# Differential attention: the squares of a head's output and their row sums on GpSimd instead of ScalarE and VectorE

## The reference, cut to what matters

```python
s = jnp.einsum('bqhcd,bkhcd->bhcqk', qb, k).astype(jnp.float32)
p = jax.nn.softmax(jnp.where(mask, s, -jnp.inf), axis=-1)
a = p[:, :, 0] - lam * p[:, :, 1]
o = jnp.einsum('bhqk,bkhe->bqhe', a.astype(v.dtype), v)      # 512 rows x 128 per head
...
o = rms_norm_2(o, subln_g) * (1.0 - lam_init)                 # per row and head: mean of 128 squares
return o.reshape(B, S, H * DIFF_V_DIM) @ w_out
```

## Time and profile before

| what | value |
|---|---|
| three runs, each one execution | 2382.07, 2386.46, 2394.81 us, median 2386.46 us |
| span of the profiled execution | 2382.2 us |
| the profiled execution's own time | no figure beside its span is given for it; the fastest run is 0.13 us under the span |
| TensorE busy | 2355.2 us, 99% of the span |
| VectorE, ScalarE, GpSimd busy | 798.0, 853.5 and 1162.4 us |
| chain that ended last, by engine | PE 88%, DVE 7%, issue 2% |
| the attention loop of the differential attention | about 1264 to 1352 us of the span |

### The profile page before, as it was taken

The page is one execution under the profiler, slowest core; times in us unless marked ns, Lnnn a source line. Parts: engine busy times, 40 slices in busy tenths (PEclk is TensorE's granted clock), DMA queues, the critical chain, the costliest instruction groups (busy, mean ns, idle before and its releaser), DMA issues.

```text
span 2382.2 us, 27151 instructions
## 1 busy us (share of the span) xinstructions
PE 2355.2 (99%) x11234; PEld 1924.9 (81%) x11234; DVE 798.0 (33%) x1384; ACT 853.5 (36%) x1266; POOL 1162.4 (49%) x960
## 2 busy tenths in 40 slices
PE   8999999999999999999999999999999999999999
PEld 7888887888887788888887678888887777788887
DVE  3222205854212322100466742022046863410210
ACT  4222214514342322212446543223156463431330
POOL 6544446634554544444452365444556822644443
PEclk9999999999999999999999999999999999999999
DMA  4323233212332323232220122233232201322322
GB/s 147 106 89 105 89 100 113 89 54 71 124 122 67 95 89 106 89 106 89 85 92 19 54 89 91 104 90 105 89 103 67 75 1 54 94 102 91 96 96 89
DMA packets 147521, 210.54 MB, mean 88 GB/s; under 512 B 6203, under 2 KB 113862, under 8 KB 147398
## 3 DMA queue, kind: packets, MB, share of 16 engines
q1 hardware_dynamic: 147398, 208.80, 27.2%
HBM read 206.69 MB, written 2.10 MB: 88 GB/s over the span
## 4 chain that ended last, share of the span: by engine, by line
PE 88%; DVE 7%; issue 2%; POOL 1%; DMA 1%; ACT 1%; SPq 0%; DVEq 0%; POOLq 0%; ACTq 0%
PE ps L1465 27%; PE ps L1467 26%; PE ps L1466 26%; PE ps L2243 2%; DVE c_work L2964 1%; DVE c_best L2963 1%; DVE small L2807 1%; PE ps L2221 1%; POOL wlo L759 1%; PE ps L2231 1%; PE ps L1726 1%; PE ps L1794 1%; POOL sq L774 1%; PE ps L1816 1%; DVE hl L2380 1%
## 5 line engine op out<-in xcount | busy, mean ns | idle before, releaser
L759 POOL TENSOR_TENSOR wlo<-raw,whi 128x512 fp32r<-128x512 f32 x776 | 1007.0, 1329 | 1082.9 <-ACT whi L952 981.8
L952 ACT ACTIVATE whi<-raw 128x2048 fp32r<-128x2048 f32 (+1 forms) x185 | 352.4, 1905 | 688.2 <-DMA raw<-in_mlp_w 317.1
L1465 PE MATMUL ps<-hh,whi 128*128 128x512 f32 x1448 | 572.9, 396 | 6.6 <-DVE hl L2380 5.4
L1467 PE MATMUL ps<-hh,wlo 128*128 128x512 f32 x1448 | 566.3, 391 | 0.0
L1466 PE MATMUL ps<-hl,whi 128*128 128x512 f32 x1448 | 566.3, 391 | 0.0
L1465 PEld LDWEIGHTS ps<-hh,whi 128*128 128x128 f32 x1448 | 273.5, 189 | 73.1 <-issue 9.3
L1467 PEld LDWEIGHTS ps<-hh,wlo 128*128 128x128 f32 x1448 | 273.3, 189 | 57.7
L1466 PEld LDWEIGHTS ps<-hl,whi 128*128 128x128 f32 x1448 | 273.7, 189 | 56.8 <-issue 1.2
L1466 PE MATMUL ps<-gl,whi 128*128 128x512 f32 x736 | 286.4, 389 | 0.0
L1465 PE MATMUL ps<-gh,whi 128*128 128x512 f32 x736 | 286.3, 389 | 0.0
L1467 PE MATMUL ps<-gh,wlo 128*128 128x512 f32 x736 | 286.3, 389 | 0.0
(11 more groups left out here) (448 smaller groups left out, 2920.1 us busy)
## 6 DMA issues: line engine op xcount, KB each, us to landing
raw<-in_mlp_w SPq DMA_DIRECT2D x64, 1024.0 KB, 5.5
raw<-in_ffn_w_up SPq DMA_DIRECT2D x22, 1024.0 KB, 5.1
raw<-in_ffn_w_down SPq DMA_DIRECT2D x22, 1024.0 KB, 4.8
raw<-in_ffn_w_gate SPq DMA_DIRECT2D x21, 1024.0 KB, 5.1
raw<-in_w_in SPq DMA_DIRECT2D x13, 1024.0 KB, 5.1
raw<-in_diff_w_in SPq DMA_DIRECT2D x12, 1024.0 KB, 5.0
raw<-in_xattn_w_kv SPq DMA_DIRECT2D x8, 1024.0 KB, 5.2
raw<-in_dsa_w_in SPq DMA_DIRECT2D x8, 1024.0 KB, 5.0
```

Source lines behind the costliest of these rows:

```text
L759: nc.gpsimd.tensor_tensor(wlo[i][:, c], raw[i][:, c], whi[i][:, c].bitcast(F32), ALU.subtract).then_inc(s_lo, 1)
L952: nc.scalar.activation(whi[i][:, 0:width(made[0])], raw[i][:, 0:width(made[0])], ACT.Copy)\
L1465: nc.tensor.matmul(dst, w_hi, x_hi, start=start, stop=False)
L1467: return nc.tensor.matmul(dst, w_lo, x_hi, start=False, stop=stop)
```

## The change

For heads 0 to 6, GpSimd makes the squares and their sums: one multiplication 128x512 of `d_o` with itself, six halving additions (256, 128, 64, 32, 16 and 8 results per partition), a seventh that leaves the four sums, and the scale to `newton`. Every one of the nine waits for the one before it. They stand ahead of `head_scaled(h)` in GpSimd's program. ScalarE's `squares` and VectorE's `row_sums` leave the loop and stay for head 7 alone, behind it. ScalarE's `factors(h)` waits for `s_dovar` as before, which GpSimd now raises.

```diff
@@ GpSimd
             def diff(b):
                 split_to(b + DIFF_BLOCKS - 1)
                 for h in range(8):
+                    if h < 7:
+                        head_squares(h)
                     head_scaled(h)
                     if h in (0, 5, 6):
                         split_to(b + DIFF_BLOCKS + (0, 5, 6).index(h))
+
+            def head_squares(h):
+
+                o, rows = d_o[:, h % 2, :], d_osq[:, :].rearrange("p (t e) -> p t e", e=P)
+                pool.wait_ge(s_dor, h + 1)
+                nc.gpsimd.tensor_tensor(d_osq[:, :], o, o, ALU.mult).then_inc(s_dosq, 1)
+                pool.wait_ge(s_dosq, 8 * h + 1)
+                n = P // 2
+                while n > 1:
+                    nc.gpsimd.tensor_tensor(rows[:, :, 0:n], rows[:, :, 0:n], rows[:, :, n:2 * n], ALU.add)\
+                        .then_inc(s_dosq, 1)
+                    pool.wait_ge(s_dosq, 8 * h + 9 - n.bit_length())
+                    n //= 2
+                nc.gpsimd.tensor_tensor(small[:, 24:28].unsqueeze(2), rows[:, :, 0:1], rows[:, :, 1:2], ALU.add)\
+                    .then_inc(s_dosq, 1)
+                pool.wait_ge(s_dosq, 8 * h + 8)
+                nc.gpsimd.tensor_scalar(newton[:, 0, 0:4], small[:, 24:28], -0.5 / P, -0.5 * EPS, ALU.mult, ALU.add)\
+                    .then_inc(s_dovar, 1)
@@ ScalarE, squares(h), now called for head 7 alone
                     act.wait_ge(s_dor, h + 1)
-                    if h:
-                        act.wait_ge(s_doss, h)
+                    act.wait_ge(s_dovar, h)
                     nc.scalar.activation(d_osq[:, :], d_o[:, h % 2, :], ACT.Square).then_inc(s_dosq, 1)
@@ ScalarE, the loop over u
                     if qt == 0 and h >= 2:
                         high(h - 2)
-                    if qt == 1 and h:
-                        squares(h - 1)
                     if qt == 2 and h:
                         factors(h - 1)
@@ VectorE, row_sums(h), now called for head 7 alone
-                    dve.wait_ge(s_dosq, h + 1)
+                    dve.wait_ge(s_dosq, 8 * h + 1)
...
-                    dve.wait_ge(s_doss, h + 1)
+                    dve.wait_ge(s_doss, 1)
@@ VectorE, the loop over u
                     if qt == 0 and h:
                         rows_copy(h - 1)
-                    if qt == 1 and h:
-                        row_sums(h - 1)
```

## The result

The changed kernel takes 2393.54 us (median of 20 runs, 2389.34 to 2395.43), the kernel before 2386.11 us (median of 20 runs beside it, 2381.81 to 2394.81). The ratio is 1.003 with a 95% interval of 1.0023 to 1.0036: slower by 5.5 to 8.6 us, less than 0.5%. The forecast was 6.6 us, and 2390.9 us.

A forecast was written before the change was run, and what follows sets the result against it. TensorE, busy 99% of the span, bounds the kernel. Head terms sum to +6.6 us on a 2382.2 us span, giving 2388.8; half the 4.3 us distance to the median makes 2390.9, range 2384 to near 2398 and 2 more.

The forecast's parts named there:

- ScalarE's part: ScalarE loses 0.62 us in seven heads; nothing is gained, as it waits for VectorE anyway.
- VectorE's part: Without row sums and scale on VectorE, the reciprocal starts earlier, limited by ScalarE's exponentials: 0.22 us gained per head.
- 4.6 us without meetings: GpSimd's nine linked operations from VectorE's rows to the raised semaphore, no collision with VectorE; lower bound 4.3 us.
- L = 5.3: GpSimd's chain length in us from VectorE's rows to the semaphore, with two d_a meetings at 0.36 us each.
- (b): Rival: GpSimd blocked for VectorE's whole instruction at every meeting; chain 5.7 to 6.07 us, +9.4 to +12 us, chance 0.18.
- L + 2.82: Time in us from VectorE's rows to TensorE's transposes: chain length, then factors 0.52, scaling 2.18, two handovers 0.12.
- L - 5.00: Change of head 3's cycle in us, repeated in heads 2 and 4, never below -0.22; forecast +0.30 each.
- +1.81: Head 1's added us: its squares start 1.11 us late behind a low part in GpSimd's program.
- L - 2.11: Head 6's added us: squares behind a low part delay ScalarE's last d_aT copy for TensorE; forecast +3.19.
- (a): Rival: short chain of 4.3 to 4.9 us, collisions of tenths; +2 to +4 us, about 2388, chance 0.25.
- (c): Rival: small dependent additions cost about 0.56 us each, chain near 7.3 us; +20.6 us, 2405, chance 0.08.
- (d): Rival: margins absorb everything, heads 1 and 6 don't pay for the low part; -1.5 us, 2383 to 2385, chance 0.04.

The follow-up runs named there:

- experiment 10: Kernel before with squares on GpSimd, sums kept on VectorE, second block's low part behind head 6's scaling; loop stretch 84.59 us, ratio to kernel before 0.9991.
- Experiment 7: Changed kernel with the halving additions of 128 to 8 results left out, a short chain; loop stretch 86.13 us, ratio to kernel before 1.0000.
- experiment 6: Changed kernel with two more dependent 128x4 operations in GpSimd's chain; loop stretch 96.63 us, ratio to kernel before 1.0061.
- experiment 4: Kernel before with first block's low part in halves behind heads 1 and 2, second's behind head 6's scaling; loop stretch 85.69 us, ratio 1.0008.
- experiment 2: Changed kernel with the first block's low part made in halves behind heads 1 and 2; loop stretch 92.04 us, ratio to kernel before 1.0036.
- experiment 1: Changed kernel with the second block's low part moved behind head 6's scaling; loop stretch 88.70 us, ratio to kernel before 1.0017.
- Experiment 9: Kernel before with only the second block's low part moved behind head 6's scaling; loop stretch 84.59 us, median 2381.62 us, ratio 0.9995.
- experiment 5: Changed kernel with only the squares on GpSimd, sums back on VectorE in the loop; loop stretch 88.24 us, ratio to kernel before 1.0003.
- experiment 8: Changed kernel with three of four low-part pieces before head 6's squares, the last behind its scaling; head 5 to 6 19.98 us, ratio 1.0034.

## Why the prediction was right

**What the change removes.** ScalarE's part at nothing: shown by experiment 10. VectorE's part at 0.22 us a head: the mechanism was right (the reciprocal ends a wait for ScalarE), its size was not. Experiment 7 shows 0.09 in heads 2 to 4 (and 0.36 in head 5), and head 0 in the changed kernel +0.02: the d_a for 128 keys meets GpSimd's scaling, a meeting that the working did not look for. It took VectorE's waits as some tenths, behind operations of 0.46 us and less, and left out the scaling, which takes 1.04.

**The chain.** 4.6 us without meetings was too long. The squares took 1.04 us and not 1.30 (both inputs are the same tensor), as the lower bound of 4.3 had it. The six additions with their gaps were sized right, at 2.58: in experiment 6, head 2, where nothing held them, they took 2.57. With the sum, the scale and the handovers that makes 4.3.

```profile
1307.01 2.57 POOL L872 TENSOR_TENSOR d_osq<-d_osq 128x256 f32<-128x256 f32 x6
```

**The meetings.** L = 5.3 was measured as 5.22 in heads 2 to 4. The two meetings came where the working put them, with the d_a for 384 and for 512 keys, but at 0.33 and 0.54 us and not at 0.36 each. So they cost 0.87 us and not 0.72, the chain without them 4.35 and not 4.6, and the two errors nearly cancel: that L came out within 0.1 us is in part luck. What a meeting cost followed from what was left of the other's instruction, less 0.13 to 0.20 us: 0.33 of 0.47 and 0.54 of 0.67 us for GpSimd in head 2, 0.58 of 0.78 for VectorE behind the scaling there, 1.12 of 1.32 in experiment 4. The Trainium skill's page "SBUF — State Buffer" (section "Who interferes with whom") states that issue order decides who blocks, and that the other is blocked for the whole instruction. The traces agree with the second part, up to those 0.13 to 0.20 us. With the first they agree in head 2; in experiment 4 VectorE's d_a started 0.05 us before GpSimd's piece by the trace and waited for it all the same. I had read that rule as a whole instruction for each meeting, rival (b); what counts is what is left of it.

**Who waits.** L + 2.82 to the transposes gives 1300.47 + 8.04 = 1308.51 in head 2; they came at 1308.81, since TensorE first had to transpose the d_a that the scaling held up. This 0.30 us, too, no step of the working had, and against it the rows come sooner after the transposes of the head before. In head 3: from rows to transposes 8.34 us for 7.82, of which 0.22 are L - 5.00 and 0.30 the d_a; from head 2's transposes to the rows 3.11 us for 3.28; together +0.35 for +0.30. Experiment 6 shows the slope of one per head in heads 3 to 6.

**Head 1.** +1.56 for +1.81; experiment 2 shows that the place caused 1.21 of it, a part of that through the meeting with the d_a for 384 keys (1.09 us in place of 0.62), which the sum had not. TensorE's wait lay elsewhere than I said: not at the transposes of d_o until GpSimd, but in two parts ahead of them, until ScalarE's exponentials, which stand behind the factors, and until the d_a for 128 keys:

```profile
1295.46 0.92 PE L1958 MATMUL ps<-a_kT,a_qT 64*128 64x384 f32 x4 [0.82 <-ACT d_p L1269]
...
1297.19 0.33 PE L1999 MATMUL ps<-ident,d_a 128*128 128x128 f32 x1 [0.82 <-DVE d_a L2837]
```

**Head 6.** +3.19 forecast, +3.43 measured, of unlike parts. From VectorE's rows the last copy is 8.12 us off (1354.61 - 1346.49) where it was 5.49 (1350.39 - 1344.90): +2.63, near L - 2.11 for the 4.85 us of this chain. The rows themselves came 0.64 us earlier after the transposes of head 5 (3.38 for 4.02): d_a for 256 keys took 0.75 us and not the 1.41 of the earlier trace rows, since the first piece of the low part had begun 0.80 us before it (1343.68 and 1344.48) and not 0.14. And the low clock added 1.44, which no step of mine had. So this term, nearly half of the sum, came near by luck.

**The signs.** The total of the chain, its two stretched operations, the reciprocal that waits for ScalarE and the gap of some 3 us in head 6 were as forecast. TensorE's 1 to 2 us of waiting in heads 1 and 5 were there in size (1.64 and 1.58), not in place. Of the signs of being wrong, "VectorE and not GpSimd stretches" came half true: both stretch, VectorE's d_a for 128 keys by 0.58 us in heads 2 to 4.

**The rivals.** (a), (b) and (c) name lengths of the chain, and the trace puts L between (a) and (b): 5.15 to 5.23 us in heads 2 to 5. (d) falls with experiments 1 and 2. **The time**: 2390.9 us is 2.6 under the median, of which 1.8 are the kernel before, set at 2384.3 where its median of 20 runs is 2386.11; on that the sum gives 2392.7. I had taken 12 us as what a measurement can tell from no change; with 20 runs each the interval is 3 us wide, and the slowdown is clear.

No version here beats the kernel before by what the runs can tell. Experiment 9's is 1 us shorter in the trace and the same in the runs.

## What to carry to other kernels

Before work moves to an idle engine, find what stands ahead of it in that engine's own program, and compute by when its last consumer must have it: here an engine idle for 9 us of each 11 us cycle had 0.47 us to spare. Then put the long, patient work (a block's low part) behind the short, awaited work; one such move gave back 3.9 of 7.0 us, 1.0 of which it gives without the change too. Count a meeting of GpSimd with VectorE's operations on two SBUF inputs at nearly what is left of the other's instruction (in these traces 0.13 to 0.20 us less), in both directions.

## What the runs showed that I had not expected

The granted clock fell to 0.50 behind an idle stretch of TensorE of 3.14 us that followed a busy loop, in experiment 5 behind one of 1.99 us with another of 0.83 us shortly before it, and in experiment 6 behind one of 1.42 us and one of 0.81 us with 0.92 us of work between them. It stayed at 1.00 behind one of 1.79 us (experiment 8) and one of 1.07 (experiment 1). So the longest idle stretch alone does not tell whether it falls. Such a wait costs more than itself: 1.44 us here and 1.63 in experiment 5.

A difference of some 0.01 us decided over 1.1 us of a cycle. In experiment 4 VectorE's d_a for 128 keys began 0.06 us before GpSimd's piece in head 1 and 0.05 us before it in head 2, and the cycles were 11.10 and 12.23 us. What decides there who waits, no run here shows.
